# A two-layer hybrid transformer step: thirteen seven-product units a layer, their products in another order, their weight sums made in pairs

## The reference

```python
def conv_ffn(h, p):
    u = h @ p['w_up']                      # (tokens, 1024) @ (1024, 2 * 2816)
    up = jnp.pad(u, ((0, 0), (pad, pad), (0, 0)))
    u = up[:, 0:t] * w[0] + up[:, 1:t + 1] * w[1] + up[:, 2:t + 2] * w[2] + p['conv_b']
    a, gt = u[..., :D_FF], u[..., D_FF:]
    return (a * jax.nn.silu(gt)) @ p['w_down']
```

## Time and profile before

| | |
|---|---|
| median of 3 runs | 2482.31 us |
| the profiled execution | 2483.54 us |
| its span | 2481.7 us |
| granted clock, mean | 0.996 |
| PE busy | 2409.0 us (97%) |
| DVE busy | 1532.7 us (62%) |
| ACT busy | 1045.6 us (42%) |
| POOL busy | 497.1 us (20%) |

### The profile page before, as it was taken

One profiled execution on the slowest core, in us unless ns is written; L12 is line 12 of the kernel. 1 busy time (PEld: TensorE's weight loads), 2 busy tenths in 40 slices (PEclk: granted clock), 3 DMA queues, 4 the chain that ended last, 5 costly groups with the idle time before them and its releaser, 6 DMA issues.

```text
span 2481.7 us, 41837 instructions
## 1 busy us (share of the span) xinstructions
PE 2409.0 (97%) x16727; PEld 2191.8 (88%) x16727; DVE 1532.7 (62%) x2732; ACT 1045.6 (42%) x1920; POOL 497.1 (20%) x418
## 2 busy tenths in 40 slices
PE   8999999999999999999999999999999999999999
PEld 6878977797799999999977799778878999999999
DVE  4675376636755864746656743776476568567474
ACT  5454255424534532524344533453254244334242
POOL 0500022032010322404104001221310104134040
PEclk9999999999999999999999999999999999999999
DMA  8212233321133223223322022321310422232322
GB/s 267 83 35 69 75 119 97 120 84 52 35 96 92 58 79 85 72 82 85 100 96 77 18 82 62 107 92 60 89 44 18 136 69 68 69 89 65 86 75 88
DMA packets 254657, 203.30 MB, mean 82 GB/s; under 512 B 10384, under 2 KB 237698, under 8 KB 254466
## 3 DMA queue, kind: packets, MB, share of 16 engines
...
q10 hardware_dynamic: 7104, 2.95, 0.4%
...
...
## 4 chain that ended last, share of the span: by engine, by line
PE 90%; DVE 4%; ACT 3%; issue 2%; POOL 0%; DMA 0%; SPq 0%; ACTq 0%; DVEq 0%; POOLq 0%
PE ps L1820 26%; PE ps L1714 16%; PE ps L1844 8%; PE ps L1736 8%; PE ps L1931 6%; PE ps L1945 4%; PE ps L1699 3%; PE ps L1701 3%; PE ps L1700 3%; PE ps L1979 3%; PE ps L1870 1%; PE ps L1571 1%; ACT prob L2233 1%; PE ps L1969 1%; PE ps L1779 1%
## 5 line engine op out<-in xcount | busy, mean ns | idle before, releaser
L2768 DVE TENSOR_TENSOR wlo<-raw,whi 128x512 fp32r<-128x512 f32 (+1 forms) x246 | 200.7, 818 | 206.2 <-ACT whi L2299 206.1
L2299 ACT ACTIVATE whi<-raw 128x512 fp32r<-128x512 f32 (+1 forms) x246 | 151.0, 615 | 297.4 <-PE ps L1820 206.0
L2515 DVE TENSOR_TENSOR wlo<-raw,whi 128x1024 fp32r<-128x1024 f32 (+2 forms) x136 | 169.0, 1243 | 171.5 <-ACT whi L2100 170.6
L2871 POOL TENSOR_TENSOR rstd<-smean,mhalf 128x4 f32<-128x4 f32 (+3 forms) x96 | 114.0, 1191 | 520.6 <-DVE smean L2576 519.8
L2100 ACT ACTIVATE whi<-raw 128x1024 fp32r<-128x1024 f32 (+2 forms) x136 | 139.2, 1023 | 179.5 <-PE ps L1714 116.4
L2604 DVE TENSOR_REDUCE negmax<-ps 128x1 f32<-128x640 f32 x192 | 151.2, 820 | 61.8 <-PE ps L1931 60.6
L2233 ACT ACTIVATE prob<-ps,negmax 128x640 f32<-128x640 f32 x192 | 150.3, 790 | 68.2 <-DVE negmax L2604 68.2
L1736 PE MATMUL ps<-hhi,whi 128*128 128x320 f32 x512 | 176.3, 344 | 1.5 <-issue 1.5
L1820 PE MATMUL ps<-hlo,whi 128*128 128x320 f32 x768 | 175.1, 309 | 0.0
L1820 PE MATMUL ps<-hhi,whi 128*128 128x320 f32 x768 | 175.0, 309 | 0.0
L1820 PE MATMUL ps<-hhi,wlo 128*128 128x320 f32 x768 | 174.9, 309 | 0.0
(11 more groups left out here) (320 smaller groups left out, 6201.0 us busy)
## 6 DMA issues: line engine op xcount, KB each, us to landing
...
```

The costliest lines, as they stand in the source:

```text
L2515: dve.tensor_tensor(dst(wlo), src, dst(whi).bitcast(F32), ALU.subtract).then_inc(S["lo_ready"], 1)
L2768: dve.tensor_tensor(ring_of(wlo, s["ring"], w), block_source(s), ring_of(whi, s["ring"], w).bitcast(F32), ALU.subtract)\
```

## The change

The change does four things, all in the MLP.

1. `SEVEN` now names units 4, 5 and 6; 0, 1, 2, 4, 5 and 6; 0, 1, 2 and 4. That is 13 a layer; in a layer there are four runs of three neighbours and one unit alone (unit 4 of the last part). Two runs follow down units (they begin a part), two follow a four-block unit.
2. `PRODUCTS` begins with a sum on row A. The copy to `wu` (now `wp6`) follows product 0, mixes follow products 1, 2, 3, 5 and 6 (before: 1, 2, 4, 5, 6), and product 6 waits for the mix of product 3 (before: of product 4). The silu of a seven-product `old` stands after the copy.
3. The four sums of a unit are made in two pairs (`part` 0 and 1), issued during the unit before: after its splits 2 and 5 where it has seven products, after its splits 0 and 1 where it has four blocks. A pair waits until its two places of `wsum` were last split. For the second pair inside a run that is `wlo5`.
4. SP's load waits for the second pair of the unit that had the slot, and no longer for the count of all sums issued.

```diff
@@ -55,13 +55,13 @@
 OFF = 512 - HALF
 FT = FF // P
 FPARTS = [(0, 8), (8, 8), (16, 6)]
-SEVEN = [(4, 6), (0, 2, 4, 6), (0, 2, 4)]
+SEVEN = [(4, 5, 6), (0, 1, 2, 4, 5, 6), (0, 1, 2, 4)]
 SUB = 1024
 BLOCK = SUB // 2
 RING = 4
 G, A = 1, 0
-PRODUCTS = (("raw", 0, G, 0, "h", 0, True, False), ("sum", 1, A, 0, "t", 1, True, True), ("sum", 0, G, 1, "t", 0, True, False),
-            ("raw", 1, G, 0, "h", 1, False, True), ("sum", 2, A, 0, "t", 2, True, False), ("sum", 3, G, 1, "h", 3, False, True),
+PRODUCTS = (("sum", 1, A, 0, "t", 1, True, False), ("raw", 0, G, 0, "h", 0, True, False), ("sum", 0, G, 1, "t", 0, True, False),
+            ("sum", 2, A, 0, "t", 2, True, False), ("raw", 1, G, 0, "h", 1, False, True), ("sum", 3, G, 1, "h", 3, False, True),
             ("raw", 3, A, 0, "t", 3, False, True))
 SUMS = ((2, 3, ALU.add), (None, 0, ALU.subtract), (0, 2, ALU.subtract), (1, None, ALU.subtract))
@@ -691,7 +691,7 @@
         ends = l + 1 == DEPTH
         wo_done = tally("sub_done")
         split_at, product_at, read_at, alo_at, load_at = [], [], {}, {}, {}
-        sums_at = [0]
+        sums_at, sum_at = {}, {}
         def load(k, after):
             if k >= len(units):
@@ -699,23 +699,29 @@
             u = units[k]
             older = units[k - 2] if k > 1 else None
             add("funit", src=u["kind"], slot=u["slot"], of=l, f0=u["f0"], nf=u["nf"], a=u["a"], lo_back=back("lo_ready", after),
-                summed=older is not None and older["seven"])
+                sum_back=back("wsum_ready", sum_at[k - 2, 1]) if older is not None and older["seven"] else None)
+
+        def sums(u, part):
+            add("wsum", slot=u["slot"], part=part, lo_back=back("lo_ready", sums_at[part]) if part in sums_at else None)
+            sum_at[u["k"], part] = tally("wsum_ready")
         def split():
             q = len(split_at)
             u, i = ring[q]
             src, j = u["blocks"][i][:2]
-            if u["seven"] and i == 0:
-                add("wsum", slot=u["slot"], lo_back=back("lo_ready", sums_at[0]) if sums_at[0] else None)
             w = BLOCK if u["kind"] == "up" else u["nf"] // 2 * P
             add("fsplit", raw=src == "raw", slot=u["slot"], off=j * w, j=j, width=w, ring=(q + ring_at) % RING,
+                sum_back=back("wsum_ready", sum_at[u["k"], j // 2] - 1 + j % 2) if src == "sum" else None,
                 sub_back=back("sub_done", product_at[q - RING] if q >= RING else wo_done))
             split_at.append(tally("lo_ready"))
             if src == "sum":
-                sums_at[0] = tally("lo_ready")
+                sums_at[j // 2] = tally("lo_ready")
             elif not any(b[0] == "raw" for b in u["blocks"][i + 1:]):
                 load(u["k"] + 2, tally("lo_ready"))
+            after = units[u["k"] + 1] if u["k"] + 1 < len(units) else u
+            if after["seven"] and i in ((2, 5) if u["seven"] else (0, 1)):
+                sums(after, (2, 5).index(i) if u["seven"] else i)
         def product():
@@ -796,15 +802,18 @@
             elif old["seven"] or old is u0:
                 conv(old, G)
                 conv(old, A)
-                silu(old)
+                if not u["seven"]:
+                    silu(old)
             else:
                 conv(old, A)
             for i in range(len(turn)):
                 product()
                 if u["seven"]:
                     if i == 0:
-                        add("wp1", pair=2 * u["s"] + G)
-                    elif i != 3:
+                        add("wp6", pair=2 * u["s"] + A)
+                        if old["seven"] or old is u0:
+                            silu(old)
+                    elif i != 4:
                         add("wmix", i=i, s=u["s"])
                 while len(split_at) < min(len(product_at) + RING, len(ring)):
                     split()
@@ -1004,9 +1013,9 @@
     if k == "fsplit":
         return dict(hi_ready=1, lo_ready=1)
     if k == "wsum":
-        return dict(wsum_ready=4)
-    if k == "wp1":
-        return dict(p1_ready=1)
+        return dict(wsum_ready=2)
+    if k == "wp6":
+        return dict(p6_ready=1)
     if k == "wmix":
         return dict(w_read=1)
     if k == "tmake":
@@ -1474,8 +1483,8 @@
                     full = S[f"raw_full{s['slot']}"]
                     r = raw[:, s["slot"], :]
                     sp.wait_ge(S["lo_ready"], n("lo_ready", -s["lo_back"]))
-                    if s["summed"]:
-                        sp.wait_ge(S["wsum_ready"], n("wsum_ready"))
+                    if s["sum_back"] is not None:
+                        sp.wait_ge(S["wsum_ready"], n("wsum_ready", -s["sum_back"]))
                     nf, f0 = s["nf"], s["f0"]
                     if s["src"] == "up":
                         for j in range(2):
@@ -1826,9 +1835,9 @@
                     block_waits(s)
                     i = s["i"]
                     if i == 3:
-                        pe.wait_ge(S["p1_ready"], n("p1_ready"))
+                        pe.wait_ge(S["p6_ready"], n("p6_ready"))
                     elif i > 3:
-                        pe.wait_ge(S["w_read"], n("w_read", -1))
+                        pe.wait_ge(S["w_read"], n("w_read", -2 if i == 4 else -1))
                     out = halves(s["pair"])[s["half"]][0]
                     wh, wl = ring_of(whi, s["ring"]), ring_of(wlo, s["ring"])
                     b = s["b"]
@@ -2294,14 +2303,14 @@
                     if s["raw"]:
                         act.wait_ge(S[full], n(full))
                     else:
-                        act.wait_ge(S["wsum_ready"], n("wsum_ready", s["j"] + 1 - len(SUMS)))
+                        act.wait_ge(S["wsum_ready"], n("wsum_ready", -s["sum_back"]))
                     act.wait_ge(S["sub_done"], n("sub_done", -s["sub_back"]))
                     act.activation(ring_of(whi, s["ring"], s["width"]), block_source(s), ACT.Copy).then_inc(S["hi_ready"], 1)
-                def wp1(s):
+                def wp6(s):
                     act.wait_ge(S["sub_done"], n("sub_done"))
                     act.wait_ge(S["w_read"], n("w_read"))
-                    act.activation(wu[:, 0, :], run(s["pair"], 0, HALF), ACT.Copy).then_inc(S["p1_ready"], 1)
+                    act.activation(wu[:, 0, :], run(s["pair"], 0, HALF), ACT.Copy).then_inc(S["p6_ready"], 1)
                 def tsplit(s):
                     act.wait_ge(S["t_made"], n("t_made"))
...
@@ -2786,13 +2795,13 @@
                 def wmix(s):
                     dve.wait_ge(S["sub_done"], n("sub_done"))
                     if s["i"] == 1:
-                        dve.wait_ge(S["p1_ready"], n("p1_ready"))
+                        dve.wait_ge(S["p6_ready"], n("p6_ready"))
                     else:
                         dve.wait_ge(S["w_read"], n("w_read"))
                     (c11, _), (c12, _) = halves(2 * s["s"] + G)
                     (c21, _), (c22, _) = halves(2 * s["s"] + A)
                     u2, u4 = wu[:, 1, :], wu[:, 2, :]
-                    out, x, p = {1: (u2, wu[:, 0, :], c21), 2: (u4, u2, c12), 4: (c22, u4, c21), 5: (c12, u2, c12), 6: (c21, u2, c21)}[s["i"]]
+                    out, x, p = {1: (u2, wu[:, 0, :], c11), 2: (u4, u2, c12), 3: (c22, u4, c21), 5: (c12, u2, c12), 6: (c21, u2, c21)}[s["i"]]
                     dve.tensor_tensor(out, x, p, ALU.add).then_inc(S["w_read"], 1)
                 def up_conv(s):
@@ -2896,9 +2905,10 @@
                     if s["lo_back"] is not None:
                         pool.wait_ge(S["lo_ready"], n("lo_ready", -s["lo_back"]))
                     r = raw[:, s["slot"], :].rearrange("p (b c) -> p b c", c=BLOCK)
-                    for i, (a, b, op) in enumerate(SUMS):
+                    for i in range(2 * s["part"], 2 * s["part"] + 2):
+                        a, b, op = SUMS[i]
                         if a is None or b is None:
-                            pool.wait_ge(S["wsum_ready"], n("wsum_ready", i if a is None else i - 1))
+                            pool.wait_ge(S["wsum_ready"], n("wsum_ready", int(a is None)))
                         x = wsum[:, 0, :] if a is None else r[:, a, :]
                         y = wsum[:, 1, :] if b is None else r[:, b, :]
                         pool.tensor_tensor(wsum[:, i, :], x, y, op).then_inc(S["wsum_ready"], 1)
```

2 lines of the change are left out of this document (1 added, 1 removed).

## The result

| | before | changed |
|---|---|---|
| median of 4 runs | 2482.58 us | 2522.59 us |
| range | 2481.68 to 2485.88 | 2520.87 to 2523.02 |
| ratio | | 1.0159 (95%: 1.0147 to 1.0171) |
| profiled execution, span | 2483.54, 2481.7 us | 2522.72, 2520.6 us |
| granted clock, mean | 0.996 | 0.992 |

The account below looks back on a forecast made before the run. TensorE was taken as the bound, busy 97% of the span. Waits of 52.0 us, less 14.1 for fewer matmuls and 3.2 for product order, gave +34.7: 2517 us against the median, range 2474 to 2538.

Parts of the forecast that it names:

- The likeliest case: Step-by-step sum of waits in runs, `va` starting late behind the second pair: 2517 us, own range 2500 to 2532, chance 0.66.
- Second units after a punctual first: Second unit of a run: second pair delays `va` and the split for the third unit, 3.5 us too long.
- after a late first: Second unit starting with four DVE steps to catch up: everything 0.9 later, so 4.4 us late.
- a rival hung (2475): Splits beside POOL cost only 0.60, so only second units are late, by 1.2 each: 2475 us, chance 0.12.
- the first unit ... 1.0 late: First unit of a run behind a four-block unit: one conv left, split at 13.3, 1.0 us late.
- First units of the second run in part 1: First unit behind a four-block unit that follows a late run: load, sums and `va` slide, 3.0 us late.
- Lone units: Unit 4 of the last part, behind a four-block unit that follows a run: 1.0 us late.
- Third units: Third unit of a run: four DVE steps to catch up, mixes late by 0.4, 0.2 and 0.7, 1.3 us.
- The clock rival: Waits in the eight second units each drop the clock, 2.2 us each, 18 us on top: 2535 us, chance 0.12.
- the clock showed 0.50 in the MLP: Sign that would show the forecast wrong: granted clock at 0.50 in the MLP of the profile after.
- 52.0: Forecast sum of all waits in seven-product units, 26.0 us a layer over two layers; may be 35 or 65.
- What I gave back for the order of products: Mix for product 6 made two products early, removing all waiting of the three longer seven-product units: 3.2 us.

Follow-up runs that it names:

- both edits: Changed kernel with the second pair behind `up_fin` inside runs and a four-block unit's pairs issued after its splits 2 and 3: 2494.0 us, 1.0054.

## Why the prediction was right, point by point

**The likeliest case came, by its mechanism.** The second pair ahead of `up_fin` set when `va` starts, and with it the split on which the next unit's product 0 waits. Moving that pair alone took 25 us off; shortening the sums took 43 off.

**The steps with their sizes.** Second units after a punctual first were put at 3.5 late and are 3.2 to 3.4; after a late first at 4.4, and are 4.4 to 4.5. `va` was forecast at 11.25 us into the unit and starts at 11.05. The hold-ups between DVE and POOL, on which a rival hung (2475), are there: the split at 995.12 takes 1.68 us beside a sum, those that POOL leaves alone 0.68. The Trainium skill (SBUF — State Buffer, two separate sides) has VectorE instructions with two SBUF inputs and GpSimd's take turns on a shared pair of ports, each for a whole instruction. The trace agrees: splits wait for sums and sums for splits (1.74 against 1.30), and mixes, with one input in PSUM, take 0.48 beside a busy POOL.

**The term that was mis-sized** is "the first unit ... 1.0 late" for part 0: it is 5.9 late, twice, 9.8 us in sum. I costed the issue of sums sooner in a four-block unit at its work on POOL only, and not at its place: the first pair of unit 4 now stands ahead of the `up_fin` of unit 1, and waits for its own load there. A step that is moved takes its waits along, and POOL's new order stood ahead of the forecast; I read it for the runs alone. Moving the pairs back brought the unit from 5.9 to 3.1. The remaining 2.1 over my 1.0 is seen in the trace of that run, whose unit starts at 855.91:

```profile
855.44 2.04 DVE L2817 SCALAR_TENSOR_TENSOR vg<-ps,PT,vg 128x127 f32<-128x127 f32 x4
...
859.98 2.04 DVE L2817 SCALAR_TENSOR_TENSOR va<-ps,PT,va 128x127 f32<-128x127 f32 x4
...
863.76 1.30 POOL L2914 TENSOR_TENSOR wsum<-raw 128x512 f32<-128x512 f32 x1 [2.53 <-DVE wlo L2777]
```

I had one conv left here and `wlo5` done 5.65 into the unit. But row G of unit 3 has slid to the unit's start as well, row A starts 4.07 in, and the second pair starts 7.85 in, 2.2 later than I had it. In the kernel before row G lay there too (854.55, the unit starts at 855.06), so the trace of before could have told it. With both edits the unit is 0.5 late. With only the second pair behind `up_fin` it is still 4.3 and 4.0 late, and with short sums, whose first pair keeps the early place and its wait for the load, 0.6. So the early place costs what it does together with POOL's time in the sums, and not by the wait for the load alone.

**Other terms were too big.** First units of the second run in part 1: 2.0 and 1.5, not 3.0 (2.5 us in sum). Lone units: on time, not 1.0 late (2.0). Third units: 0.84 where the clock stayed, not 1.3 (3.7 over eight). On-time second units: 0.8. Together 9.0 us down against 9.8 up, and the clock on top.

**The clock rival came in part.** It had each of eight waits cost 2.2 us, 18 in all. The windows (busy of PE, PEld, DVE, ACT, POOL; granted clock; DMA share; GB/s) behind the wait at 1002.48 and behind one at 1061.53 of the same length:

```profile
1002.50:1005.50 3.00, 3.00 (x12) 3.00 (x13) 3.00 (x7) 1.77 (x2) 0.00 (x0) 0.54 0.00 0
...
1061.50:1064.50 3.00, 2.97 (x20) 2.97 (x21) 3.00 (x7) 1.87 (x3) 0.00 (x0) 1.00 0.00 0
```

In the first PE runs 12 matmuls in 3 us at about half clock (1.2 of 2.4 GHz), in the second 20 at full clock. Of ten waits of 2.6 to 2.7 us ahead of a unit's product 0 seven ended in such a stretch of 3.4 us, three did not; at the shorter ones in these units, of 1.8 us and less, there was none. The fall of the earlier trace rows is a weaker witness for a fall behind a wait than I took it for: the clock reads 0.50 from 1258.0 on, and the wait of 1.77 us there ends only at 1259.56, so the fall came with its beginning. The price was small: six third units with a fall are 1.50 to 1.64 late, the two without 0.84, so 0.66 to 0.80 each and 4.6 us in sum; the second unit with one is 4.45 late, the one without 4.46. I had said the forecast would be wrong if the clock showed 0.50 in the MLP, which was too strong. Half speed for 3.4 us would be 1.7 us, but where a unit waits for DVE anyway, slow matmuls first use up that wait: the 0.31 us before product 4 in the unit from 1061.53 is gone in the one from 1002.48. Between its matmuls the first unit has 0.84 us of waits, large and small; the second is 1.64 late by its slow matmuls alone. The Trainium skill (TensorE: Matmul & The Clock Gate, HAM oscillation) lets each burst behind a long enough wait begin at half clock; the trace shows it in seven of ten and puts its price here at a third of what I had from the earlier trace rows, where the half clock lasts 6.8 us and not 3.4.

**The sum again.** 52.0 + 9.8 - 9.0 + 4.6 is 57.4, where 57.5 was measured (late second units were 0.1 too small). The forecast of 2517 is 5.6 us under 2522.6, inside the range that the step-by-step case was given.

**What I gave back for the order of products** was 3.2 us. As a sum that was right, for the old late units are gone from the list; as a reason it was not. The mix that is ready sooner is worth 0.7 us without the runs.
